# Mixture-of-experts loop: transposes of the activated tile issued ahead of the last two depth slices of the next expert's gate product

## What is computed

```python
def expert_block(args):
    xblk, e = args
    hid = jax.nn.silu(xblk @ w_gate[e]) * (xblk @ w_up[e])
    return hid @ w_down[e]

yb = lax.map(expert_block, (xb, block_e))
y = jnp.zeros((n_tok + 1, d), f32).at[buf_t].add(yb.reshape(cap, d).astype(f32) * buf_g[:, None])
```

## Time and profile before

| | |
|---|---|
| median of 3 runs | 2773.99 us |
| lowest, highest | 2769.28, 2774.26 us |
| span of the profiled execution | 2770.1 us (the page has no other time of it) |
| TensorE busy | 2617.0 us, 94% |
| VectorE busy | 1563.2 us, 56% |
| ScalarE busy | 1318.0 us, 48% |
| mean granted TensorE clock | 0.986 of full speed |
| low halves of weights in the experts (VectorE, line 2671) | 192 of 2286 ns |
| casts of weights in the experts (ScalarE, line 2575) | 192 of 1912 ns |

### The profile page before, as it was taken

The page is one execution under the profiler, slowest core; times in us unless marked ns, Lnnn a source line. Parts: engine busy times, 40 slices in busy tenths (PEclk is TensorE's granted clock), DMA queues, the critical chain, the costliest instruction groups (busy, mean ns, idle before and its releaser), DMA issues. The chain is left out here.

```text
span 2770.1 us, 66149 instructions
## 1 busy us (share of the span) xinstructions
PE 2617.0 (94%) x28073; PEld 2190.7 (79%) x28073; DVE 1563.2 (56%) x2377; ACT 1318.0 (48%) x2272; POOL 316.2 (11%) x367
## 2 busy tenths in 40 slices
PE   6999999999999999989999999999999999999992
PEld 5989897777766766678999998888888888888882
DVE  4566664443035555544444444553326888888884
ACT  4645552222134444334444444552223777777771
POOL 0111222332000000001212121100001000000002
PEclk9999999999999999999999999999998999999996
DMA  4344332222132323313221201154345999999976
GB/s 111 148 167 145 125 138 89 92 93 74 37 96 65 99 68 102 114 38 81 55 69 52 64 21 33 48 152 129 121 185 219 397 395 395 395 396 395 395 301 258
DMA packets 162649, 440.53 MB, mean 159 GB/s; under 512 B 16295, under 2 KB 96825, under 8 KB 150097
## 3 DMA queue, kind: packets, MB, share of 16 engines
q1 hardware_dynamic: 146413, 381.95, 38.7%
q10 hardware_dynamic: 9060, 29.56, 2.8%
q0 software_dynamic: 6912, 25.17, 2.4%
HBM read 344.22 MB, written 92.41 MB: 158 GB/s over the span
## 5 line engine op out<-in xcount | busy, mean ns | idle before, releaser
L2671 DVE TENSOR_TENSOR ex_wL<-wx,ex_wH 128x2048 fp32r<-128x2048 f32 x192 | 436.1, 2286 | 46.5 <-ACT ex_wH L2575 43.8
L2575 ACT CAST ex_wH<-wx 128x2048 fp32r<-128x2048 f32 x192 | 366.4, 1912 | 96.3 <-PE ex_bank L2467 70.7
L2465 PE MATMUL ex_bank<-ex_wH,ex_xTH 128*128 128x512 f32 x512 | 199.4, 389 | 0.6 <-DVE ex_xTL L2676 0.6
L2467 PE MATMUL ex_bank<-ex_wL,ex_xTH 128*128 128x512 f32 x512 | 199.3, 389 | 0.0
L2466 PE MATMUL ex_bank<-ex_wH,ex_xTL 128*128 128x512 f32 x512 | 199.2, 389 | 0.0
L717 PE MATMUL ph_acc<-ph_wH,uH 128*104 128x512 f32 x480 | 191.5, 399 | 0.0
L717 PE MATMUL ph_acc<-ph_wH,uL 128*104 128x512 f32 x480 | 188.8, 393 | 0.0
L717 PE MATMUL ph_acc<-ph_wL,uH 128*104 128x512 f32 x480 | 188.6, 393 | 0.0
L419 PE MATMUL pf_acc<-uH,pf_wH 128*128 128x348 f32 x648 | 160.7, 356 | 6.4 <-DVE pf_wL L541 6.4
L419 PE MATMUL pf_acc<-uL,pf_wH 128*128 128x348 f32 x648 | 138.9, 323 | 0.0
L419 PE MATMUL pf_acc<-uH,pf_wL 128*128 128x348 f32 x648 | 138.3, 322 | 0.0
(11 more groups left out here) (416 smaller groups left out, 6879.5 us busy)
## 6 DMA issues: line engine op xcount, KB each, us to landing
wx<-in_expert_w_gate SPq DMA_DIRECT2D x32, 2048.0 KB
wx<-in_expert_w_up SPq DMA_DIRECT2D x32, 2048.0 KB
wx<-in_expert_w_down SPq DMA_DIRECT2D x32, 2048.0 KB
s_y<-ex_y ACTq DMA_DIRECT2D x32, 512.0 KB, 10.0
fw<-in_w_in SPq DMA_DIRECT2D x27, 512.0 KB
hw<-in_w_in SPq DMA_DIRECT2D x6, 2048.0 KB, 10.1
s_qkT<-ph_stg ACTq DMA_DIRECT2D x4, 2080.0 KB, 7.0
mb_gt<-s_pT SPq DMA_DIRECT2D x16, 512.0 KB, 3.6
```

The costliest lines, as they stand in the source:

```text
L2465: nc.tensor.matmul(out, aH, bH, start=first, stop=False)
L2467: return nc.tensor.matmul(out, aH, bL, start=False, stop=last)
L2575: nc.scalar.copy(wH[:, w, part], raw(j, s)[:, part]).then_inc(w_high, 1)
L2671: nc.vector.tensor_tensor(wL[:, w, part], raw(j, s)[:, part], wH[:, w, part], ALU.subtract).then_inc(w_low, 1)
```

## The change

`into_hidden` and `gate` take a range of depth slices. In the loop, and for the last pair after it, the gate product of expert `n + 1` is issued in two pieces, slices 0 to 5 ahead of `turn_h(n)` and slices 6 and 7 behind it. The waits for the two weight halves stay at slices 0 and 4, and the counts of `w_used` at slices 3 and 7. The same bank is accumulated into before and after the transposes. `up`, the first gate product and the overflow path issue as before.

```diff
         GATE_BANK = (2, 7)
+        EARLY = 6
         UP_BANK = 3
...
-        def into_hidden(pe, out, s, r, w):
-            for h in range(2):
-                pe.wait_ge(w_low, 2 * r + h + 1 + OPEN)
-                for k in range(4 * h, 4 * h + 4):
-                    last = three(out, xTH[:, s, k, :], xTL[:, s, k, :], wH[:, w, k * FF:(k + 1) * FF],
-                                 wL[:, w, k * FF:(k + 1) * FF], k == 0, k == KD - 1)
-                last.then_inc(w_used, 1)
-
-        def gate(pe, s, n, r, w):
-            pe.wait_ge(x_low, n + 1 + OPEN)
-            pe.wait_ge(mixed, n - 1 + OPEN)
-            into_hidden(pe, bank[:, GATE_BANK[s], :], s, r, w)
+        def into_hidden(pe, out, s, r, w, ks=range(KD)):
+            for k in ks:
+                if k % 4 == 0:
+                    pe.wait_ge(w_low, 2 * r + k // 4 + 1 + OPEN)
+                last = three(out, xTH[:, s, k, :], xTL[:, s, k, :], wH[:, w, k * FF:(k + 1) * FF],
+                             wL[:, w, k * FF:(k + 1) * FF], k == 0, k == KD - 1)
+                if k % 4 == 3:
+                    last.then_inc(w_used, 1)
+
+        def gate(pe, s, n, r, w, ks=range(KD)):
+            if ks[0] == 0:
+                pe.wait_ge(x_low, n + 1 + OPEN)
+                pe.wait_ge(mixed, n - 1 + OPEN)
+            into_hidden(pe, bank[:, GATE_BANK[s], :], s, r, w, ks)
...
-                    gate(pe, 1 - s, n + 1, rank(G, n + 1), s)
+                    gate(pe, 1 - s, n + 1, rank(G, n + 1), s, range(EARLY))
                     turn_h(pe, n)
+                    gate(pe, 1 - s, n + 1, rank(G, n + 1), s, range(EARLY, KD))
                     turn_x(pe, s, n + 2, i + 1)
...
-            gate(pe, 1, n + 1, rank(G, n + 1), 0)
+            gate(pe, 1, n + 1, rank(G, n + 1), 0, range(EARLY))
             turn_h(pe, n)
+            gate(pe, 1, n + 1, rank(G, n + 1), 0, range(EARLY, KD))
```

## The result

| | before | changed |
|---|---|---|
| median | 2773.76 us (4 runs) | 2744.21 us (4 runs, 2740.07 to 2745.74) |
| span of the profiled execution | 2770.1 us | 2741.1 us |
| ratio | | 0.9897, 95% interval 0.9885 to 0.9909 |

The direction and the mechanism held, the size did not. About 24 us of it lie in the experts, the rest ahead of them, where nothing was changed.

The account below looks back on a forecast made before the run. TensorE was taken to set the pace, with loads following. Cutting the period from 18.59 to 17.95 us gave 29 x 0.64 + 0.65 - 0.07 = 19.1 us, so 2774.0 - 19.1 = 2754.9 us, range 2748 to 2764.

Parts of the forecast that it names:

- The stall: Before `project`, TensorE waits 0.77 us per period for VectorE's `low_h`; moving six gate matmuls behind `turn_h` removes it.
- The margin of the multiply: At the earlier `turn_h`: its input `mixed` is ready 0.30 us before, cost 0; lateness beyond that is paid in full.
- TensorE's floor: TensorE's own work per expert, from `project` to `project`: 17.82 us, plus 0.13, making the new period 17.95 us.
- the passage: One more switch on TensorE from float32 transposes to matmuls, behind `turn_h`: costs 0.13 us per period, bounds 0 and 0.26.
- VectorE's floor: VectorE's chain per expert through the down low half and `low_h` to `project`: 17.84 us, 0.75 less than before.
- First and last turns: Ends of the expert loop: the first moved turn comes 0.07 us later, the last gains 0.65 us.
- The DMA rival: Weight transfers in the expert loop become the bound: period 18.4 us, gain 5.7 us, time 2768.3 us; chance 8%.
- The other two rivals: Another wait, on VectorE's chain, replaces the stall: near 2773 us, 8%; late `mixed` holds `turn_h` and gate matmuls: 2788, 4%.

Follow-up runs that it names:

- the second study: Both kernels, unchanged, profiled and timed once more: medians 2764.9 us before and 2740.2 us changed, ratio 0.9912.

## Why the prediction was wrong, and where it was right

- **The stall, its cause and its end**: right. The recurring wait of `project` went, with `move_h`'s 1.28 us and `low_h`'s 0.75. Its size was not 0.77 but 0.86 us, since the eight transposes ahead of it take 0.80 and not 0.90 (below).
- **The margin of the multiply** (0.30 us, each microsecond beyond paid in full): right. One slice fewer takes it away, and the period loses 0.57.
- **TensorE's floor, "17.82 + 0.13 = 17.95"**: this is the step that failed. It measured 17.735, 0.215 less, of which 0.08 is in the four transposes (0.39 for 0.47), 0.11 in the eight (0.79 for 0.90), and some 0.03 in `project` and the six matmuls. The spacing of transposes that are followed by others, or by a stall, was taken for the whole block's price, and 0.13 put on top for the passage. The matmuls behind the transposes did cost that (1.48 for six instead of 1.36), but the block's last transpose gives back 0.08 to 0.10 of it. The stage before had it in its timeline, one row ahead of those I read the earlier trace rows: eight transposes at 1990.77 and the matmul at 1991.56, which is 0.79, against the 0.90 that I worked out inside a stalled group. Over 29 periods the term is 29 x 0.215 = 6.2 us, and the gain by the periods 29 x 0.855 = 24.8, where the forecast had 29 x 0.64 = 18.6. The row of the kernel before:

```profile
1990.77 1.03 PE L2213 MATMUL or_bank<-ident,or_u 128*128 128x128 f32 x8
```

- **VectorE's floor, "17.84"**: too high by the same kind of slip. Rows of that engine overlap by 0.08 us, and I added a listed length (2.28) where the next starts after 2.20. That makes the sum 17.76; the kernel ran at 17.735, with `project` at 5.55 instead of 5.57, which stands in this chain too. Had only TensorE's term been right, this one would still have put the period 0.1 too high.
- **First and last turns** (0.07 lost, 0.65 won): small, as forecast, but not sure to a microsecond. From the end of the first multiply to the first `project` it is 2.96 us before, 2.96 in the second profile of the changed kernel and 4.22 in the first, where the clock fell to 1.2 GHz after `turn_h`'s wait and the six moved matmuls stood behind it. The last moved turn won 0.86 (17.63 for 18.49). From the first `project` to that of expert 30 the gain is 25.2 and 25.6 us; the rest of the blocks, ahead of it and behind, differs by up to 2 us between two profiles of either kernel, and so the two pairs of blocks give 23.7 and 26.2, with a mean of 25.0.
- **The rest of the 29.5 us**, about 5, is no effect of the change: it lies ahead of the experts, in unchanged stages, and the second study, with other executions of both kernels, has 24.7. The range allowed 3 us for that. With both floors at what was measured the forecast would have been 2754.9 - 6.2 = 2748.7, just within the range, and the scatter alone would have put the time near 2750; the two errors together left it.
- **The DMA rival** was refuted: at 414 GB/s no cast waits for a load, though its arithmetic took 399 for the most that a share of 0.99 allows. The limit of 358 GB/s for HBM in the Trainium skill (DMA: Bandwidth & Descriptors, Specifications) does not bind here; 414 stays below the 435 it gives for the fabric. The other two rivals have no trace in the waits.

## What to carry to other kernels

Where an engine waits on a chain that starts from its own output, issue that output as early as its input exists, and put independent work behind it; how early is set by two rows, the end of the input and the end of the cover, and here one slice to either side costs 0.17 or 0.57 us per turn. Price a block of instructions by the distance from its first start to the start of what follows, at a place where it is followed by the same kind and nothing stalls; lengths, group means and spacings inside a stalled group don't add up to that. To judge a step of a few microseconds in a kernel whose executions scatter by ten, compare periods or the length of the stage.

## What the runs showed that I had not expected

- The passage from float32 transposes to matmuls is free to 0.02 us on TensorE: the first matmul starts 0.03 to 0.04 us after the last transpose, and its successor comes 0.31 us later instead of 0.23.
- Transposes followed by transposes of another tile take 0.47 us for four, against 0.39 ahead of a matmul.
- A DMA share of 0.99 at 395 GB/s was not a full set of engines: the same mix of transfers ran at 414, with a share of 1.01. Here the share did not tell what rate was left.
- A memset of 0.09 us between two VectorE instructions cost nothing, one of 0.38 cost 0.34. Why the small one vanishes is open.
- The start of the experts' stage moved by 10 us between two executions of the same kernel (2075.3 and 2085.0), while the stage itself kept its length to 0.6 us (685.7 and 685.1).
- Six matmuls now stand behind the first turn's wait, and what the clock did there varied: with the same 2.46 us of idle time ahead of `turn_h` in the first turn, `project` followed 2.96 us after the multiply in one profile of the changed kernel and 4.22 in the other.
